# First feed-forward of a two-block transformer kernel: weights become the stationary operand, the tokens' two parts stream past side by side

## The reference, cut to what matters

```python
hf = rmsnorm(x, g_ff[l])
x = x + jnp.square(jax.nn.relu(hf @ w_ff1[l])) @ w_ff2[l]     # w_ff1: 2048 x 8192, w_ff2: 8192 x 2048
```

## Time and profile before

| what | value |
|---|---|
| median of 3 runs | 2686.72 us (2685.83 to 2688.96) |
| the profiled execution | 2688.03 us, span 2686.3 us, mean granted clock 0.997 |
| TensorE matmul busy | 2658.2 us (99%) in 12304 matmuls |
| VectorE, ScalarE, GpSimd busy | 1709.7, 1122.8, 7.4 us |
| DMA | 483.61 MB, mean 180 GB/s |

### The profile page before, as it was taken

One profiled execution on the slowest core, in us unless ns is written; L12 is line 12 of the kernel. 1 busy time (PEld: TensorE's weight loads), 2 busy tenths in 40 slices (PEclk: granted clock), 3 DMA queues, 4 the chain that ended last, 5 costly groups with the idle time before them and its releaser, 6 DMA issues.

```text
span 2686.3 us, 33948 instructions
## 1 busy us (share of the span) xinstructions
PE 2658.2 (99%) x12304; PEld 2207.9 (82%) x12304; DVE 1709.7 (64%) x2519; ACT 1122.8 (42%) x1469; POOL 7.4 (0%) x43
## 2 busy tenths in 40 slices
PE   9999999999999999999999999999999999999998
PEld 7978888888878888888888888877888888888887
DVE  7678765576777565655566686776665555555555
ACT  4333454434343333333333644444444444434432
POOL 0000000000000000000000000000000000000000
PEclk9999999999999999999999999999999999999999
DMA  7655556555545555555555565544455555555554
GB/s 221 182 157 165 157 158 219 195 182 185 181 141 185 194 185 196 184 189 188 195 186 196 173 205 159 150 133 126 157 186 193 192 192 191 188 189 192 190 189 154
DMA packets 262353, 483.61 MB, mean 180 GB/s; under 512 B 17722, under 2 KB 38900, under 8 KB 261876
## 3 DMA queue, kind: packets, MB, share of 16 engines
q1 hardware_dynamic: 261956, 482.10, 56.2%
q10 hardware_dynamic: 304, 0.27, 0.0%
HBM read 480.22 MB, written 2.10 MB: 180 GB/s over the span
## 4 chain that ended last, share of the span: by engine, by line
PE 96%; DVE 3%; ACT 1%; issue 0%; DMA 0%; DVEq 0%; ACTq 0%
PE bank L974 30%; PE bank L976 30%; PE bank L975 30%; PE bank L1048 3%; PE bank L1011 1%; DVE w_split L1130 1%; PE bank L1081 1%; PE bank L1064 1%; PE bank L1058 0%; PE bank L1083 0%; PE bank L1016 0%; ACT act_junk L798 0%; PE bank L965 0%; DMA xres<-in_x 0%; PE bank L1077 0%
## 5 line engine op out<-in xcount | busy, mean ns | idle before, releaser
L812 ACT ACTIVATE w_split<-w_raw 128x1024 fp32r<-128x1024 f32 (+2 forms) x920 | 960.2, 1046 | 1284.6 <-PE bank L976 1236.5
L1130 DVE TENSOR_TENSOR w_split<-w_raw,w_split 128x1024 fp32r<-128x1024 f32 (+2 forms) x920 | 1084.2, 1203 | 251.1 <-ACT w_split L812 244.8
L974 PE MATMUL bank<-w_split,act_a_hi 128*128 128x512 f32 (+2 forms) x2400 | 948.4, 395 | 4.1 <-DVE w_split L1130 4.0
L976 PE MATMUL bank<-w_split,act_a_lo 128*128 128x512 f32 (+2 forms) x2400 | 927.9, 387 | 0.0
L975 PE MATMUL bank<-w_split,act_a_hi 128*128 128x512 f32 (+2 forms) x2400 | 926.1, 386 | 0.0
L974 PEld LDWEIGHTS bank<-w_split,act_a_hi 128*128 128x128 f32 x2400 | 453.2, 189 | 89.4 <-DVE w_split L1130 5.0
L976 PEld LDWEIGHTS bank<-w_split,act_a_lo 128*128 128x128 f32 x2400 | 452.4, 188 | 89.1
L975 PEld LDWEIGHTS bank<-w_split,act_a_hi 128*128 128x128 f32 x2400 | 453.9, 189 | 81.9
L974 PE MATMUL bank<-w_split,act_b_hi 128*128 128x512 f32 x1248 | 492.0, 394 | 3.2 <-issue 2.9
L976 PE MATMUL bank<-w_split,act_b_lo 128*128 128x512 f32 x1248 | 487.7, 391 | 0.0
L975 PE MATMUL bank<-w_split,act_b_hi 128*128 128x512 f32 x1248 | 487.2, 390 | 0.0
(11 more groups left out here) (183 smaller groups left out, 950.5 us busy)
## 6 DMA issues: line engine op xcount, KB each, us to landing
w_raw<-in_w_ff SPq DMA_DIRECT2D x256, 512.0 KB, 4.4
w_raw<-in_w_in SPq DMA_DIRECT2D x208, 512.0 KB, 3.8
w_raw<-in_w_gate SPq DMA_DIRECT2D x88, 512.0 KB, 4.1
w_raw<-in_w_up SPq DMA_DIRECT2D x88, 512.0 KB, 4.5
w_raw<-in_w_down SPq DMA_DIRECT2D x88, 512.0 KB, 4.6
w_raw<-in_w_out SPq DMA_DIRECT2D x64, 512.0 KB, 4.0
w_raw<-in_w_in SPq DMA_DIRECT2D x24, 368.0 KB, 3.4
w_raw<-in_w_dsa_o SPq DMA_DIRECT2D x16, 512.0 KB, 4.9
```

The source lines that it names most:

```text
L812: nc.scalar.activation(whi[:, s, 0:w], raw[:, s, 0:w], ACT.Copy).then_inc(hi_ready, 1)
L974: pe.matmul(o, hi[:, cols], rhs_hi, start=k == 0, stop=False)
L976: ins = pe.matmul(o, lo[:, cols], rhs_hi, start=False, stop=k == c["kt"] - 1)
L1130: v_e.tensor_tensor(wlo[:, s, 0:w], raw[:, s, 0:w], whi[:, s, 0:w].bitcast(F32), ALU.subtract).then_inc(lo_ready, 1)
```

## The change

The up chunks of the first feed-forward get the weights as the stationary operand. For each `k` tile and each of the four blocks `f` of 128 features, one matmul streams both parts of the tokens (2x256 columns, high and low side by side) past the high weights, and one streams the high part (256 columns) past the low weights into the right half of the same bank. An up chunk so fills four banks (0 to 3 for the first of a pair, 4 to 7 for the second), with its left half holding one part of the sum and its right half the other, and with features on the partitions. No transpose follows. A chain of four parts `U` takes the place of the drain and the two steps `T`: ScalarE copies the four right halves to `stage`, VectorE adds the left halves and computes `max(u,0)*u`, ScalarE rounds that to `act_b_hi`, VectorE subtracts for `act_b_lo`. The `rstd` is no longer applied there; `rstd_sq`, its square, multiplies the product in the drain of the down chunks. Up chunks take no number `c` any more. The down chunks of the loop move to the banks 4 to 7 (`bank0=4`), and each up chunk waits for what last used its banks.

```diff
@@ plan
+def weave_up(c, side, start):
+    return weave(c, side, start)[:-1]
...
     def up(i, half, **more):
-        return gemm("w_ff1", 0, (2 * i + half) * CH, KT, "A", ev="relu2", rstd="h", step=(0, 2 * CH), rows=True, **more)
-
-    fa, fb = up(0, 0, need=filled(hf)), up(0, 1)
-    seq += weave(fa, pend + [("rstd", dict(of="x", name="h"))], 2)
-    ta = turns(fa, "B", 0)
-    seq += weave(fb, ta, 3)
+        return gemm("w_ff1", 0, (2 * i + half) * CH, KT, "A", step=(0, 2 * CH), kind="up", half=half, **more)
+
+    def activated(c):
+        return [("U", dict(chunk=c, part=i)) for i in range(4)]
+
+    fa, fb = up(0, 0, need=filled(hf), banks_of=mo[2:4]), up(0, 1, banks_of="aux")
+    seq += weave_up(fa, pend + [("rstd", dict(of="x", name="h", square=True))], 2)
+    seq += weave_up(fb, activated(fa), 1)
     segments = [(seq, 1)]
     body = []
-    tb = turns(fb, "B", 4)
-    fa, fb2 = up(1, 0), up(1, 1)
-    body += weave(fa, tb, 3)
-    down_need = filled(ta + tb)
-    for m in range(4):
-        body += weave(gemm("w_ff2", 0, m * CH, 8, "B", 0, need=down_need if m == 0 else (), ev="addx", off=m * CH,
-                           step=(2 * CH, 0)))
-    ta2 = turns(fa, "B", 0)
-    body += weave(fb2, ta2, 2)
+    fa, fb2 = up(1, 0, banks_of="up"), up(1, 1)
+    body += weave_up(fa, activated(fb), 1)
+    downs = [gemm("w_ff2", 0, m * CH, 8, "B", 0, need_up=[(0, fb)] if m == 0 else (), ev="addx", off=m * CH, scaled=True, bank0=4,
+                  step=(2 * CH, 0)) for m in range(4)]
+    for c in downs:
+        body += weave(c)
+    fb2["banks_of"] = downs[2:4]
+    body += weave_up(fb2, activated(fa), 1)
...
-    tb = turns(fb2, "B", 4)
+    ub = activated(fb2)
...
-    seq += [a0, b0, tb[0], a1, tb[1], b1, distances[0], a2, distances[1], a3, ("E", down[0]), b2, distances[2], b3, ("E", down[1])]
+    seq += [a0] + ub[:2] + [b0] + ub[2:] + [a1, b1, distances[0], a2, distances[1], a3, ("E", down[0]), b2, distances[2], b3, ("E", down[1])]
@@ ScalarE
+            def activated(what, turn):
+                half = what["chunk"]["half"]
+                u = stage[:, half].rearrange("p t c -> p (t c)")
+                if what["part"] == 0:
+                    wait(act_e, group_done, what["end"], turn.g)
+                    for f in range(4):
+                        ins = nc.scalar.activation(u[:, f * SEQ:(f + 1) * SEQ], bank[4 * half + f][:, SEQ:2 * SEQ], ACT.Copy)
+                    ins.then_inc(up_lows, 1)
+                elif what["part"] == 2:
+                    wait(act_e, up_squared, what["v"] + 1, turn.v)
+                    nc.scalar.activation(act["B"][0][:, half * 4 * SEQ:(half + 1) * 4 * SEQ], u, ACT.Copy).then_inc(up_hi, 1)
@@ TensorE
+            def up_group(c, i, s, turn):
+                of = c["banks_of"]
+                if i == 0 and of == "up":
+                    wait(pe, up_out, c["v"] - 1, turn.v)
+                elif i == 0 and of == "aux":
+                    for j in (c["last_j"] - 1, c["last_j"]):
+                        pe.wait_ge(aux_out[j % 2], j // 2 + 1)
+                for f in range(4):
+                    if i == 0 and f % 2 == 0 and not isinstance(of, str):
+                        for x in of:
+                            if x["c"] % 2 == f // 2:
+                                wait(pe, chunk_out[x["c"] % 2], x["c"] // 2 + 1, turn.c2)
+                    o = bank[4 * c["half"] + f]
+                    for kk in range(2):
+                        k = 2 * i + kk
+                        w = slice(kk * CH + f * P, kk * CH + (f + 1) * P)
+                        both, hi = act_a[:, :, k * SEQ:(k + 1) * SEQ], act_a[:, 0, k * SEQ:(k + 1) * SEQ]
+                        pe.matmul(o[:, :].rearrange("p (s t) -> p s t", s=2), whi[:, s, w], both, start=k == 0, stop=False)
+                        ins = pe.matmul(o[:, SEQ:2 * SEQ], wlo[:, s, w], hi, start=False, stop=k == KT - 1)
+                ins.then_inc(group_done, 1)
...
-                        o = prod_bank[par * 2 + t][:, 0:c["n"]]
+                        o = bank[c.get("bank0", 0) + par * 2 + t][:, 0:c["n"]]
@@ VectorE
-                        ins = v_e.tensor_tensor(x, b[t], x, ALU.add)
+                        if c.get("scaled"):
+                            ins = v_e.scalar_tensor_tensor(x, b[t], s_("rstd_sq", t, t + 1), x, ALU.mult, ALU.add)
+                        else:
+                            ins = v_e.tensor_tensor(x, b[t], x, ALU.add)
...
-                elif ev == "relu2":
-                    for t in range(NT):
-                        ins = v_e.tensor_scalar(stage[:, s, t, :], b[t], r[t], 0.0, ALU.mult, ALU.max)
-                    ins.then_inc(out_sem, 1)
-                    wait(dve, out_sem, out_n, turn.c2)
-                    v_e.tensor_tensor(stage[:, s], stage[:, s], stage[:, s], ALU.mult).then_inc(rows_ready, 1)
...
+            def activated(what, turn):
+                half, v = what["chunk"]["half"], what["v"] + 1
+                u = stage[:, half].rearrange("p t c -> p (t c)")
+                if what["part"] == 1:
+                    wait(dve, up_lows, v, turn.v)
+                    for f in range(4):
+                        uf = u[:, f * SEQ:(f + 1) * SEQ]
+                        ins = v_e.tensor_tensor(uf, bank[4 * half + f][:, 0:SEQ], uf, ALU.add)
+                    step(ins)
+                    v_e.scalar_tensor_tensor(u, u, 0.0, u, ALU.max, ALU.mult).then_inc(up_squared, 1)
+                elif what["part"] == 3:
+                    hi, lo = (x[:, half * 4 * SEQ:(half + 1) * 4 * SEQ] for x in act["B"])
+                    wait(dve, up_hi, v, turn.v)
+                    v_e.tensor_tensor(lo, u, hi.bitcast(F32), ALU.subtract).then_inc(up_out, 1)
...
+                    if what.get("square"):
+                        step(v_e.tensor_tensor(s_("rstd_sq"), s_("rstd_h"), s_("rstd_h"), ALU.mult))
```

More of the change, by code:

```diff
@@ L282, in up @@
     def up(i, half, **more):
-        return gemm("w_ff1", 0, (2 * i + half) * CH, KT, "A", ev="relu2", rstd="h", step=(0, 2 * CH), rows=True, **more)
-    fa, fb = up(0, 0, need=filled(hf)), up(0, 1)
-    seq += weave(fa, pend + [("rstd", dict(of="x", name="h"))], 2)
-    ta = turns(fa, "B", 0)
-    seq += weave(fb, ta, 3)
+        return gemm("w_ff1", 0, (2 * i + half) * CH, KT, "A", step=(0, 2 * CH), kind="up", half=half, **more)
[4 more added lines that the diff above has]
+    seq += weave_up(fb, activated(fa), 1)
     segments = [(seq, 1)]
     body = []
-    tb = turns(fb, "B", 4)
-    fa, fb2 = up(1, 0), up(1, 1)
-    body += weave(fa, tb, 3)
-    down_need = filled(ta + tb)
-    for m in range(4):
-        body += weave(gemm("w_ff2", 0, m * CH, 8, "B", 0, need=down_need if m == 0 else (), ev="addx", off=m * CH,
-                           step=(2 * CH, 0)))
-    ta2 = turns(fa, "B", 0)
-    body += weave(fb2, ta2, 2)
+    fa, fb2 = up(1, 0, banks_of="up"), up(1, 1)
[6 more added lines that the diff above has]
+    body += weave_up(fb2, activated(fa), 1)
     turns_ff = FF // (2 * CH)
     segments.append((body, turns_ff - 1))
-    tb = turns(fb2, "B", 4)
+    ub = activated(fb2)
     seq = [("load_gain", {})]
     distances = [("distances", dict(part=i)) for i in range(8)]
-    down = [gemm("w_ff2", (turns_ff - 1) * 2 * CH, m * CH, 8, "B", 0, need=filled(ta2 + tb) if m < 2 else (),
-                 ev="addx", off=m * CH, rows=True) for m in range(4)]
+    down = [gemm("w_ff2", (turns_ff - 1) * 2 * CH, m * CH, 8, "B", 0, need_up=[(0, fa), (2, fb2)] if m == 0 else (),
+                 ev="addx", off=m * CH, scaled=True, rows=True) for m in range(4)]
     xt = [turn("x", 2 * i * P, "A", 2 * i, down[i // 2], gain="attn_norm_2", nth=i + 1) for i in range(8)]
@@ L423, in number @@
                 if what["i"] == 0 and c["kind"] != "cmp":
-                    take(c, "c")
+                    take(c, "v" if c["kind"] == "up" else "c")
                     mine.append(c)
+                    if c["kind"] == "up" and c["banks_of"] == "aux":
+                        c["last_j"] = n["j"] - 1
                 take(what, "g")
@@ L428, in number @@
                 what["need_j"] = [x["ref_j"] for k, x in c["need"] if k in tiles]
+                what["need_v"] = [x["ref_v"] + 1 for i, x in c.get("need_up", ()) if i == what["i"]]
                 s = what["g"] % RING
@@ L431, in number @@
                 groups.append(dict(chunk=c, i=what["i"], landed=landed[s], width=GROUP if c["kind"] == "cmp" else c["gk"] * c["n"]))
-                c["end"] = what["g"] + 1
+                c["end"] = c["ref_end"] = what["g"] + 1
+            elif kind == "U":
+                what["end"], what["v"] = what["chunk"]["ref_end"], what["chunk"]["ref_v"]
             elif kind in "TPOXCV":
@@ L465, in number @@
                         what["ref_" + k] += per[k] * (reps - 1)
+                if "ref_end" in what and (id(what), "end") not in seen:
+                    seen.add((id(what), "end"))
+                    what["ref_end"] += per["g"] * (reps - 1)
```

(14 more changed lines are left out.)

15 lines of the change are left out of this document (9 added, 6 removed).

## The result

The changed kernel takes 2704.07 us (median of 4 runs, 2701.51 to 2704.65) against 2687.19 us for the kernel before in the same comparison: ratio 1.0063, 95% interval 1.0051 to 1.0075, so 16.9 us slower. Forecast were +10.2 us, 2697 us, and a range of 2688 to 2705. The span of the profiled execution is 2702.7 us, 16.4 us longer than before. The difference in the span is complete by the end of the first feed-forward: TensorE's first wait in the second block, 2.6 us long in both, ended at 1545.86 us and ends at 1562.31.

The account below looks back on a forecast made before the run. TensorE, busy 99% of the span, was taken to bound the kernel. Matmuls +6.8, transposes -15.4, waits +12.5 and +4.6, and clock +1.7 gave +10.2 us on 2686.72: 2697 us, range 2688 to 2705.

Parts of the forecast that it names:

- The wait at the second up chunk: First matmul of fb2 in each loop turn waits for the newest down chunk's drain: 1.79 us, 7 times, +12.5 us.
- The wait at the first up chunk: Before the loop, fa waits for the drain of mo[3], delayed by two steps T: +4.6 us, once.
- The clock: Clock falls to 1.2 GHz after the first up chunk's wait, +1.7 us (0 to 2.8); nothing for the loop's seven waits.
- The rival of a clock that falls in each turn: Clock falls at each loop wait too, up to 1.7 us each, +11.9: 2709 us; chance 0.09.
- the choice between two near rows: No clock loss at the loop's 1.79 us waits: 2.01 us idle kept the clock, 2.09 behind eight transposes lowered it.
- The transposes: 32 steps T behind the up chunks go, 0.48 us each: -15.4 us (bounds -14.1 and -16.0).
- The chain `U`: Copies, additions and rounding after up chunks stay hidden from TensorE; at the loop's end by only 0.9 us.
- The matmuls: Up groups take 2.773 us instead of 2.720, with 120 ns per 256-column matmul: +6.8 us (bounds +5.8 and +9.9).
- The sign named in the forecast: Matmul pair starts 0.347 us apart in up groups; 0.36 would mean the weight load is not fully covered (+13 us).
- The sum: All terms together +10.2 us, 2697 us; low bounds together +5.1, 2692, high ones +16.9, 2703.6.
- its chances for "slower": Whole kernel slower by over 0.2% (above 2692.1 us): 0.71 from the forecast plus rivals, in sum 0.84.

Follow-up runs that it names:

- forder: The changed kernel with up-chunk blocks taken in the order f = 2, 3, 0, 1; 2691.78 us, ratio 1.0018 to the kernel before.
- t_one: The kernel before, with only the first of four transposes in each of 32 steps T behind the first feed-forward's up chunks; 2676.01 us against 2686.34.
- eight run: forder_mo with a group's eight wide matmuls before its eight narrow ones (first group block by block), newest drain's two banks waited for singly; 2680.26 us, ratio 0.9980.
- halfw2: The changed kernel with 64 instead of 128 weight columns in the wide matmuls of all but each up chunk's first group; 2694.08 us in one run.
- contig: The changed kernel with wide matmuls streaming 512 adjacent high-part columns instead of two separate stretches, in every up chunk but the first; 2701.3 us, ratio 1.0053.
- wide512: The changed kernel with the narrow matmuls also given 512 columns, so no narrow stream remains; 2804.49 us in one run.
- forder_mo: forder with the drain of mo[3] put ahead of the two steps T that stood before it; 2687.14 us, ratio 1.0001 to the kernel before.

## Why the prediction was right, and by how much it was off

*The wait at the second up chunk.* Right in place, releaser, number and size: 7 x 1.77 = 12.4 us against 12.5. The profile shows it, and forder moves it by the 1.4 us of two blocks. The forecast came from the numbers of the chunks: the last down chunk of a turn is always even, and the first block asks for the even one.

*The wait at the first up chunk.* Right: 4.7 us against 4.6. From the start of the eight transposes to the second matmul of the chunk were 1.10 us (794.70 to 795.80), and are 5.77 (794.49 to 800.26).

*The clock.* In the first feed-forward it fell once, after the 4.42 us, and not at the seven waits of the loop in any of the five runs that have them (1.50 us without a matmul, 1.93 without a load). In the three runs without the first chunk's wait it doesn't fall there. At 1.2 GHz a pair takes 0.64 instead of 0.354; of the 3.4 us at that level (PEclk 0.83 over 10 us is 1.7 us short, at half speed) about 1.5 are lost, against 1.7. The rival of a clock that falls in each turn is refuted, and the choice between two near rows came out as made: the idle time of 2.09 us that did bring it down had eight transposes ahead of it, these have large matmuls on both sides. Whether that is the reason, or only the shorter time without a matmul, no run tells apart.

*The transposes.* 15.4 us forecast. t_one shows 10.3 for three quarters of them. All of them are not measured by themselves; with the waits, the clock and the pairs as measured, they are what is left of the 16.7 us by which the stretch from the eight transposes (794.70 and 794.49) to the end of the first wait in the second block (1545.86 and 1562.31) grew: 13.6 + 12.4 + 4.7 + 1.5 - 16.7 = 15.5 us.

*The chain `U`.* Hidden, as forecast. There is no wait of TensorE for it, and at the end of the loop, where 0.9 us of room were reckoned, the copies of the four banks took 1.19 us and the four additions 1.42 where four times 0.47 and four times 0.42 were reckoned.

*The matmuls: this term was mis-sized.* The step that failed is "8 x 0.2267 + 8 x 0.120 = 2.773 us", 347 ns a pair and +6.8 us in all: it took the load of the wide matmul as covered ("0.11 us for 128 columns, just under the 0.12 us of the 256-column matmul that must cover it") and the wide matmul as no slower next to narrow ones than among its like. Measured are 353, +13.6 us (1024 x 353.3 = 361.8 us, less 128 x 2.720 = 348.2), beyond the high bound of +9.9. That is 6.8 us, about the whole distance from the forecast (16.9 against 10.2 in the median). The 120 ns of the narrow one were right (117); the wide one costs 236 and not 227. The sign named in the forecast, a pair of 0.36 us if the load is not fully covered, came out half way. The runs show what stands in its place: with half of the weight columns under the wide matmul the pair is 340, with wide streams only it is 453 as two ordinary ones, and with narrow streams and full loads 347 to 353, where the same instructions hold either value for a whole chunk. Shown is that the excess needs both the narrow streams and the full width of the weights; that the load comes late is the likely mechanism, with the two numbers of the eight run against it as the whole account. Why the pattern is 353 in one chunk and 347 in another, and 348 in another order, stays open. The row of 119 ns with 64 weight columns and the straight line through 352 columns gave the narrow one rightly; no row of before had a wide one between narrow ones.

*The sum.* The low bounds add up to +5.3 and the high ones to +16.7, not to +5.1 and +16.9 as the forecast has it, and its chances for "slower" to 0.85 instead of 0.84; neither changes the forecast. The measured 2704.07 lies at the upper edge of the range, 2688 to 2705, and above the high bounds' 2703.6. That the range held is partly luck: one term left its bounds, and the range was just wide enough.

The Trainium skill ("TensorE: Matmul & The Clock Gate", Back-to-back issue gap) says of a stream of loads and matmuls that "the per-MM spacing is set by *both* ops". The halfw2 run fits this: 340 ns instead of 353 for the same streams with a shorter load. The same section's figure of about 131 ns for 512 columns is not what this case shows, 226.7 ns.

So the change does win what it removes, and gives back more than that: +13.6 for narrow matmuls, +12.4 and +6.2 (with the clock) for the waits at the second up chunks and at the first. With the waits mended it is even with the kernel before (2687.14 against 2686.66), and with the matmuls grouped and the last bit of the wait gone it is 5.6 us faster (2680.26 against 2685.84).

## What to carry to other kernels

When a producer is given more banks and the consumer's banks are moved beside them, ask of the first matmul which drain it waits for: the newest cost the whole drain and a restart (1.77 us here). Begin with the bank that has been free longest, which here left 0.37 us. When one orientation trades matmuls of 512 columns for pairs of 512 and 256 at the same total of columns, expect the pair to cost more than the two spacings read elsewhere: here 353 ns, or 348 in the better order, where 340 were reached with half the weight columns. Look for side work in front of a drain in the drain's own queue; two steps of conversions there made a wait of 4.7 us where the drain alone would have cost an estimated 1.8, as in the loop, and the clock came down besides.

## What the runs showed of the hardware that was not expected

A stream of alternating wide and narrow matmuls can run at two paces with the same instructions, 347 or 353 ns a pair, and keeps its pace for the whole chunk (contig run, the only one that has the quick pace). In the slow one, three pairs form a period of 1.06 us, with one pair of 0.36 us and two of 0.35. With full loads, wide ones in a stream that also has narrow ones take 230 to 236 ns on average even where a wide one stands ahead, while in a stream of wide ones only (the down chunks, wide512) they take 227. A wait of TensorE with large matmuls on both sides, 1.50 us without one, once in 90 us, never brought its clock down, 35 times in five runs; 4.42 us (the changed kernel) and 2.9 us (forder) did.

Between them lies a length that does either. At the start of the second block TensorE waits 2.5 to 2.6 us in every version. In seven of the eleven profiled executions the clock fell to 1.2 GHz for 3.4 us there, in four it did not. The windows view around it, the kernel before in the first fence and forder_mo in the second:

```profile
1540.00:1550.00 10.00, 7.43 (x27) 5.69 (x26) 7.52 (x23) 2.12 (x2) 0.00 (x0) 0.83 0.48 142
```

```profile
1541.00:1551.00 10.00, 7.46 (x35) 5.80 (x34) 8.18 (x22) 2.20 (x3) 0.00 (x0) 1.00 0.53 159
```

0.17 of 10 us is 1.7 us less of full-speed work in one execution than in another. That may be part of the 3 to 4 us by which the times of one version differ; it isn't shown.
